# Expert rows added one pair behind their dots, and every fourth row of the first two chunks added by VectorE

## The chip, the cores and the metric

One core of a Trainium2 chip runs the whole program as one launch. The metric is the device time of one execution in microseconds. TensorE (PE in the profile) multiplies matrices, VectorE (DVE) and ScalarE (ACT) work on rows of 128 partitions, GpSimd (POOL) here only issues gathers, SyncE (SP) loads weights and stores the last result.

## The reference

Three layers on 512 tokens of width 1024, all in float32: a block with a short convolution and a block with a state-space mixer, each with a SwiGLU network, and then a hybrid layer: band attention and a gated delta rule side by side, and behind them a layer of retrieved experts (`peer`). The change concerns `peer` alone. For each token, 8 heads rank two sets of 128 keys, keep the 16 best sums each, and so name 128 experts out of 16384. Each expert is one pair of rows of 1024 numbers, `expert_down` and `expert_up`:

```
act = gelu(einsum("thkd,td->thk", expert_down[experts], hb))
y   = einsum("thk,thkd->td", gates * act, expert_up[experts])
out = x + gate2 * y
```

Tokens are handled in 4 chunks of 128. So there are 4 x 128 = 512 "rows" of work: row n = 128 c + s is the s-th expert of every token of chunk c, one expert per partition.

## The kernel before, in words

Everything ahead of the experts runs first. The hybrid layer is done in two halves of 256 tokens. Its second half (`main`, the generators `pe_main`, `act_main`, `dve_main` with f = 1) is cut into steps and woven into the expert loop, and so is the ranking of the keys for the next chunk (`ranks`, `dve_topk`): `steps_of` takes one or two steps of each a group. In chunk 0 that is one main step and two ranking steps, in chunk 1 one main step until these are used up and from then on a ranking step, in chunk 2 a ranking step, in chunk 3 none.

**One row.** `pool_gather` issues an indirect DMA of 128 x 2048 numbers (1 MB: the down and the up row of one expert for each token) into a slot. `dve_dots` multiplies the down half with the tokens' h (`htk`) and sums it, one custom instruction (L187), into a column of `dots`. `act_gelu` applies the gelu to both columns of a group (a group is GG = 2 rows, "a pair"). `dve_gate` multiplies with the gates (L170, 128x2). `act_diag` makes a 128x128 diagonal matrix of the result from the identity (L164, 128x128), one of 8 buffers. `pe_add` multiplies this matrix with the up half and adds it in PSUM (`acc`), two instructions in the code of 512 columns each, which the profile shows as four matmul records a row (L153, psum<-tail,arena 128x512).

**Slots.** For rows 0 to 255 there are NRING = 7 slots, from row 256 on 12, since memory of the main program has come free. A row's gather waits until TensorE has added the row that had the slot before (`g_mm.at(prev[n])`), 7 or 12 rows earlier.

**Order.** Every engine runs its own list; all wait by semaphores. Of one group, before the change:

```
VectorE: dve_dots(g)  steps_of(g)  dve_gate(g)
ScalarE: act_gelu(g)  steps_of(g)  act_diag(g)
TensorE:              steps_of(g)  pe_add(g)
```

At the end of a chunk `pe_finish` broadcasts the layer's gate (`gB`) and transposes x (`xo`) into PSUM, `act_finish` copies `gB` to `fin_out`, `dve_finish` multiplies it with `acc` and adds `xo`, and `store` writes it out (ScalarE for chunks 0 to 2, in the next chunk's group 4; SyncE for the last).

Helper lines carry all instructions: L153 matmul, L158 transpose, L164 activation, L170 tensor_tensor, L176 and L177 tensor_scalar, L182 scalar_tensor_tensor, L187 the dot, L216 the gather. "tail" is the memory of the hybrid layer (slots, dots, `fin_out`), "arena" holds among others the diagonal matrices and x.

Of the kernel before, what the change touches and what calls it, by code (L numbers as in the profile page):

```python
# [226 lines left out]
def build(nc, t, out):  # L227
    ctx = ExitStack()
    with ctx:
# [970 lines left out]
        def wait_steps(n):  # L1200
            for _ in range(n):
                yield
# [783 lines left out]
        def pe_tok(e, c):  # L1986
            for u in range(2):
                key = "htk", c, u
                o = ps.claim(key, QGB)
                e.wait_ge(*ps.vacant(key))  # L1990
                e.wait_ge(*t_h.at((5, c // 2, 7)))
                for k in range(4):
                    ins = e.tr(o[:, part[k]], H[:, 4 * u + k, part[c % 2]], ident)
                ins.then_inc(*tk_pe.tick((c, u)))
                yield
            yield

        def act_tok(e, c):
            yield
            for u in range(2):  # L2000
                e.wait_ge(*tk_pe.at((c, u)))
                if c > 1:
                    e.wait_ge(*g_dot.at(128 * (c - 2) + 127))
                e.act(htk[c % 2][:, 512 * u:512 * u + 512], ps["htk", c, u], ACT.Copy).then_inc(*ps.release(("htk", c, u)))
                yield
# [14 lines left out]
        def act_topk(e, c):  # L2020
            yield from wait_steps(31)
            e.wait_ge(*k_dve.at((c, "gate_in")))
            e.act(gates[c % 2], gates[c % 2], ACT.Exp).then_inc(*k_gate.tick(c))
            yield
# [130 lines left out]
        for n in range(512):  # L2155
            prev.append(last_use.get(slot_no[n]))
            last_use[slot_no[n]] = n
        g_in = landed("expert_landed", len(SLOTS))
        stored = landed("stored", 2)

        def pool_gather(e):
            for n in range(512):
                c, i = n // 128, n % 128
                e.wait_ge(*idx_ok.at(c))
                if prev[n] is not None:
                    e.wait_ge(*g_mm.at(prev[n]))
                e.gather(SLOTS[slot_no[n]], t["experts"], eidx[c % 2][:, i:i + 1]).then_inc(
                    *g_in.tick((c, i), slot_no[n]))

        def dve_dots(e, c, grp):  # L2170
            n = 128 * c + GG * grp
            d = dots[(n // GG) % 8]
            e.wait_ge(*ps.done(("htk", c, 1)))
            if n >= 8 * GG:
                e.wait_ge(*g_diag.at(n - 7 * GG - 1))
            for i in range(GG):
                s = SLOTS[slot_no[n + i]]
                e.wait_ge(*g_in.at((c, GG * grp + i)))
                e.ttr(s[:, 0:1024], s[:, 0:1024], htk[c % 2], d[:, i:i + 1]).then_inc(*g_dot.tick(n + i))
# [8 lines left out]
        def act_gelu(e, c, grp):  # L2188
            n = 128 * c + GG * grp
            d = dots[(n // GG) % 8]  # L2190
            e.wait_ge(*g_dot.at(n + GG - 1))
            e.act(d, d, ACT.Gelu).then_inc(*g_gelu.tick(n))

        def act_diag(e, c, grp):
            n = 128 * c + GG * grp
            d = dots[(n // GG) % 8]
            e.wait_ge(*g_act.at((c, grp)))
            for i in range(GG):
                if n + i >= 8:
                    e.wait_ge(*g_mm.at(n + i - 8))  # L2200
                e.act(diag[(n + i) % 8], ident, ACT.Copy, scale=d[:, i:i + 1]).then_inc(*g_diag.tick(n + i))

        def pe_add(e, c, grp):
            for i in range(GG):
                s_i = GG * grp + i
                n = 128 * c + s_i
                if s_i == 0:
                    for u in range(2):
                        ps.claim(("acc", c, u), (u,))
                        e.wait_ge(*ps.vacant(("acc", c, u)))  # L2210
                e.wait_ge(*g_in.at((c, s_i)))
                e.wait_ge(*g_diag.at(n))
                for u in range(2):
                    ins = e.mm(ps["acc", c, u], diag[n % 8], SLOTS[slot_no[n]][:, 1024 + 512 * u:1536 + 512 * u],
                               s_i == 0, s_i == 127)
                ins.then_inc(*g_mm.tick(n))

        def pe_finish(e, c):
            for u in range(2):
                o = ps.claim(("gB", c, u), HB)  # L2220
                e.wait_ge(*ps.vacant(("gB", c, u)))
                e.wait_ge(*der_ok.at((5, "post")))
                for k in range(4):
                    ins = e.mm(o[:, part[k]], post(5, 4 * u + k).broadcast_to([128, 128]), ident)
                ins.then_inc(*f_pe.tick(("gB", c, u)))
                o = ps.claim(("xo", c, u), HB)
                e.wait_ge(*ps.vacant(("xo", c, u)))
                for k in range(4):
                    ins = e.tr(o[:, part[k]], xT[:, 4 * u + k, 128 * c:128 * c + 128], ident)
                ins.then_inc(*f_pe.tick(("xo", c, u)))  # L2230

        def act_finish(e, c):
            for u in range(2):
                e.wait_ge(*f_pe.at(("gB", c, u)))
                if c:
                    e.wait_ge(*stored.at((c - 1, u)))
                e.act(fin_out[:, 512 * u:512 * u + 512], ps["gB", c, u], ACT.Copy).then_inc(*ps.release(("gB", c, u)))

        def dve_finish(e, c):
            e.wait_ge(*g_mm.at(128 * c + 127))  # L2240
            for u in range(2):
                f = fin_out[:, 512 * u:512 * u + 512]
                e.wait_ge(*ps.done(("gB", c, u)))
                e.tt(f, ps["acc", c, u], f, ALU.mult).then_inc(*ps.release(("acc", c, u)))
            for u in range(2):
                f = fin_out[:, 512 * u:512 * u + 512]
                e.wait_ge(*ps.done(("acc", c, u)))
                e.wait_ge(*f_pe.at(("xo", c, u)))
                e.tt(f, ps["xo", c, u], f, ALU.add).then_inc(*ps.release(("xo", c, u)))

        def store(e, c):
            for u in range(2):
                e.wait_ge(*ps.done(("xo", c, u)))
                e.dma(out[0, 128 * c:128 * c + 128, 512 * u:512 * u + 512], fin_out[:, 512 * u:512 * u + 512]).then_inc(
                    *stored.tick((c, u), u))
# [10 lines left out]
        def steps_of(c, grp, main, ranks):  # L2266

            if c == 0:
                some(ranks, 2)
                some(main, 2 if grp % 4 == 3 else 1)  # L2270
            elif c == 1 and next(main, True) is None:
                pass
            else:
                some(ranks, 1)

        def pe_experts(e):
            main = pe_main(e, 1)
            before_rows(main, iter(()))
            for c in range(4):
                ranks = iter(()) if c == 3 else wait_steps(32)  # L2280
                late = pe_tok(e, 3) if c == 2 else iter(())
                for grp in range(GROUPS):
                    steps_of(c, grp, main, ranks)
                    next(late, None)
                    pe_add(e, c, grp)
                pe_finish(e, c)

        def act_experts(e):
            main = act_main(e, 1)
            before_rows(main, iter(()))  # L2290
            drive(act_topk(e, 0))
            for c in range(4):
                ranks = iter(()) if c == 3 else act_topk(e, c + 1)
                late = act_tok(e, 3) if c == 2 else iter(())
                for grp in range(GROUPS):
                    act_gelu(e, c, grp)
                    steps_of(c, grp, main, ranks)
                    next(late, None)
                    if c and grp == 4:
                        store(e, c - 1)  # L2300
                    act_diag(e, c, grp)
                act_finish(e, c)

        def dve_experts(e, ranks):
            main = dve_main(e, 1)
            before_rows(main, ranks)
            drive(ranks)
            for c in range(4):
                ranks = iter(()) if c == 3 else dve_topk(e, c + 1)
                late = wait_steps(3) if c == 2 else iter(())  # L2310
                for grp in range(GROUPS):
                    dve_dots(e, c, grp)
                    steps_of(c, grp, main, ranks)
                    next(late, None)
                    dve_gate(e, c, grp)
                dve_finish(e, c)

# [228 lines left out]
```

## Time and profile before

| what | value |
|---|---|
| median of 3 runs | 3680.81 us (3666.36 to 3682.61) |
| the profiled execution | 3679.49 us, span 3677.7 us |
| PE busy | 3141.4 us (85%) |
| DVE busy | 2043.9 us (56%) |
| ACT busy | 1178.7 us (32%) |
| gathers | 512, 536.90 MB, first issued at 2100.36 us, last at 3640.8 us |
| row 0 dotted | 2106.76 us |
| row 128 dotted | 2656.70 us |
| row 256 dotted | 3032.26 us |

Times are microseconds from the start of the span. The expert loop takes up the last 1,578 us. Busy shares are those of an engine in a stretch; the idle time ahead of an instruction is given with what ended it. "DMA" is the mean busy share of the core's 16 DMA engines.

### The profile page before, as it was taken

The numbers are of one execution on the slowest core, as the hardware profiler recorded it, in microseconds if no ns is written. First come the engines' busy times: TensorE is split into PE (matmuls) and PEld (weight loads), VectorE is DVE, ScalarE is ACT, GpSimd is POOL, SyncE is SP. The second block draws the span as 40 slices with busy tenths as digits, with TensorE's granted clock in tenths as the row PEclk, the third lists the DMA queues.
The fourth block names the chain that finished last, engine by engine and source line by source line (L and its number), as shares of the span: only waits on it lengthen the run. The fifth ranks groups of instructions, "written<-read, shape, count | busy, mean of one in ns | idle before, by whom it ended". The sixth has DMA issues, their size and how long they took to land.

```text
span 3677.7 us, 34267 instructions
## 1 busy us (share of the span) xinstructions
PE 3141.4 (85%) x12402; PEld 2158.0 (59%) x12402; DVE 2043.9 (56%) x3974; ACT 1178.7 (32%) x2171; POOL 562.0 (15%) x540
## 2 busy tenths in 40 slices
PE   6989999798777989998988888977999777777777
PEld 4868888586555868886777635654565233223222
DVE  6654443776555454432552797554444878855554
ACT  3243222433444342223732345621222122211111
POOL 0000000000000000000000022212333444443332
PEclk9999999898888999998999989999999999999999
DMA  6534444242111424442303476867898999999998
GB/s 219 189 114 147 145 139 137 78 139 81 40 43 44 132 92 146 142 136 86 103 24 103 146 293 232 308 227 258 337 364 341 409 417 421 422 421 421 421 421 336
DMA packets 147543, 797.81 MB, mean 217 GB/s; under 512 B 16304, under 2 KB 18480, under 8 KB 81712
## 3 DMA queue, kind: packets, MB, share of 16 engines
q0 software_dynamic: 73728, 536.90, 36.8%
q1 hardware_dynamic: 69840, 251.69, 21.0%
q10 hardware_dynamic: 3808, 7.02, 0.5%
q8 instruction: 101, 1.65, 0.2%
q14 instruction: 66, 0.54, 0.0%
HBM read 793.46 MB, written 2.10 MB: 216 GB/s over the span
## 4 chain that ended last, share of the span: by engine, by line
PE 65%; DMA 17%; DVE 11%; ACT 4%; issue 3%; another core or an unknown queue 0%; POOL 0%; DVEq 0%; SPq 0%; ACTq 0%; POOLq 0%
PE psum L153 64%; DMA tail<-in_experts,tail 16%; DVE tail L187 2%; ACT arena L164 2%; DVE arena L182 2%; DVE tail L170 1%; ACT L164 1%; DVE tail L193 1%; PE psum L158 1%; DVE region L170 1%; DVE tail L190 1%; ACT region L164 1%; ACT tail L164 0%; DVE rounded L182 0%; DVE tail L196 0%
## 5 line engine op out<-in xcount | busy, mean ns | idle before, releaser
L153 PE MATMUL psum<-tail,arena 128*128 128x512 f32 (+2 forms) x3916 | 1386.7, 507 | 306.8 <-ACT arena L164 284.1
L153 PE MATMUL psum<-rounded,rounded 128*128 128x512 f32 x5496 | 1293.6, 396 | 40.1 <-DVE rounded L182 27.3
L153 PEld LDWEIGHTS psum<-tail,arena 128*128 128x128 f32 x3916 | 738.4, 196 | 916.8 <-issue 860.4
L153 PEld LDWEIGHTS psum<-rounded,rounded 128*128 128x128 f32 x5496 | 1036.6, 190 | 280.0 <-issue 56.2
L216 POOL DMA_INDIRECT tail<-in_experts,tail x512 | 541.9, 1058 | 1949.0 <-PE psum L153 977.9
L187 DVE CUSTOM_DVE_ANT_0 tail<-tail 128x1024 f32<-128x1024 f32 x512 | 621.4, 1225 | 351.7 <-DMA tail<-in_experts,tail 346.9
L170 DVE TENSOR_TENSOR rounded<-arena,rounded 128x1024 fp32r<-128x1024 f32 (+2 forms) x285 | 316.4, 1111 | 346.6 <-ACT rounded L164 346.4
L164 ACT ACTIVATE rounded<-arena 128x1024 fp32r<-128x1024 f32 (+2 forms) x317 | 291.9, 939 | 446.2 <-DVE arena L170 238.9
L164 ACT ACTIVATE tail<-tail 128x2 f32<-128x2 f32 (+1 forms) x288 | 64.1, 223 | 659.3 <-DVE tail L187 657.6
L164 ACT ACTIVATE arena<-arena,tail 128x128 f32<-128x128 f32 x512 | 177.6, 395 | 293.6 <-DVE tail L170 291.7
L164 ACT ACTIVATE arena<-psum 128x256 f32<-128x256 f32 (+2 forms) x210 | 97.8, 482 | 512.3 <-PE psum L153 512.0
L153 PE MATMUL psum<-arena 128*128 128x1 f32 (+3 forms) x792 | 197.6, 375 | 75.3 <-ACT arena L164 45.2
L164 ACT ACT_TABLE_LOAD x180 | 230.9, 1283 | 11.7 <-PE psum L153 6.4
L182 DVE SCALAR_TENSOR_TENSOR arena<-arena 128x512 f32<-128x512 f32 (+1 forms) x294 | 212.3, 724 | 21.7 <-ACT arena L164 10.9
L153 PEld LDWEIGHTS psum<-arena 128*128 128x128 f32 x792 | 127.5, 206 | 126.0 <-issue 82.1
L170 POOL TENSOR_TENSOR region<-region 128x256 f32<-128x256 f32 x24 | 19.9, 829 | 1130.6 <-DVE region L170 1130.6
L153 PE MATMUL psum<-tail 128*128 128x128 f32 (+4 forms) x888 | 138.9, 304 | 20.6 <-DVE tail L182 18.6
L153 PEld LDWEIGHTS psum<-tail 128*128 128x128 f32 (+2 forms) x888 | 108.8, 186 | 51.8 <-DVE tail L182 25.7
L170 DVE TENSOR_TENSOR arena<-psum,arena 128x512 f32<-128x512 f32 (+1 forms) x88 | 41.6, 476 | 168.2 <-PE psum L153 167.9
L182 DVE SCALAR_TENSOR_TENSOR arena<-psum,arena 128x511 f32<-128x511 f32 (+3 forms) x112 | 79.8, 713 | 97.2 <-PE psum L153 51.1
L170 DVE TENSOR_TENSOR tail<-tail 128x2 f32<-128x2 f32 (+5 forms) x299 | 95.7, 321 | 60.4 <-ACT tail L164 49.6
L164 ACT ACTIVATE arena<-arena 128x512 f32<-128x512 f32 (+3 forms) x138 | 80.6, 598 | 89.6 <-DVE arena L170 29.3
(82 smaller groups left out, 1452.5 us busy)
## 6 DMA issues: line engine op xcount, KB each, us to landing
arena<-in_ada SPq DMA_DIRECT2D x136, 512.0 KB
arena<-in_fin SPq DMA_DIRECT2D x88, 512.0 KB
arena<-in_win SPq DMA_DIRECT2D x56, 512.0 KB
arena<-in_fout SPq DMA_DIRECT2D x32, 512.0 KB
arena<-in_mxbc SPq DMA_DIRECT2D x32, 512.0 KB
arena<-in_pq SPq DMA_DIRECT2D x32, 512.0 KB
arena<-in_ain SPq DMA_DIRECT2D x24, 512.0 KB
arena<-in_mz SPq DMA_DIRECT2D x16, 512.0 KB
```

What stands on the lines that cost most here:

```text
L153: return self.e.matmul(o, a, b, start=start, stop=stop, skip_group_check=skip)
L158: return self.e.transpose(o, a, ident)
L164: return self.e.activation(o, a, func, bias=bias, scale=scale)
L170: return self.e.tensor_tensor(o, a, b, op)
L182: return self.e.scalar_tensor_tensor(out=o, in0=a, scalar=s, in1=b, op0=op0, op1=op1)
L187: return self.e.tensor_tensor_reduce(o, a, b, 1.0, 0.0, ALU.mult, ALU.add, total)
L190: return Unissued() if self.e is None else self.e.max(o, a)
L193: return Unissued() if self.e is None else self.e.max_index(o, m, a)
L216: return self.e.indirect_dma_start(out=o, out_offset=None, in_=table, in_offset=bass.IndirectOffsetOnAxis(ap=rows, axis=0))
```

## The change

Two things are done at once. First, `dve_gate`, `act_diag` and `pe_add` are called for the group before the one whose dots and steps are due, over chunk borders too, and on VectorE and ScalarE ahead of the steps. Second, `own_add(n)` names rows that VectorE adds itself: from slot 24 of a chunk on, every fourth row (s % 4 == 1) of chunks 0 and 1, and every sixteenth (s % 16 == 9) of chunks 2 and 3: 26, 26, 7 and 7 rows. It multiplies the up half with the column of `dots` and adds it to `fin_out` (`dve_add`, one scalar_tensor_tensor of 128x1024; the first of a chunk a tensor_scalar). The finish sums `acc` and `fin_out`, multiplies with `gB` straight from PSUM, and adds `xo`; `act_finish` is gone. The order of one group is now:

```
VectorE: dve_dots(g)  dve_gate(g-1)  dve_add(g-1)  [dve_finish(c-1) in a chunk's group 1]  steps_of(g)
ScalarE: act_gelu(g)  act_diag(g-1)  [store]  steps_of(g)
TensorE: steps_of(g)  pe_add(g-1)    [pe_finish(c-1) in a chunk's group 0]
```

The diff, cut to its core:

```diff
+        g_own = signal("expert_added_own")
+        def own_add(n):
+            s = n % 128
+            return s >= 24 and (s % 4 == 1 if n < 256 else s % 16 == 9)
+        by_pe = [n for n in range(512) if not own_add(n)]
+        turn = {n: i for i, n in enumerate(by_pe)}
+        added = lambda n: g_own.at(n) if own_add(n) else g_mm.at(n)
...
-                    e.wait_ge(*g_mm.at(prev[n]))
+                    e.wait_ge(*added(prev[n]))
...
+        def dve_add(e, c, grp):
+            for i in range(GG):
+                n = 128 * c + GG * grp + i
+                if not own_add(n):
+                    continue
+                v, g = SLOTS[slot_no[n]][:, 1024:2048], dots[(n // GG) % 8][:, i:i + 1]
+                e.wait_ge(*g_act.at((c, grp)))
+                before = [m for m in range(128 * c, n) if own_add(m)]
+                if before:
+                    e.wait_ge(*g_own.at(before[-1]))
+                    e.stt(fin_out, v, g, fin_out, ALU.mult, ALU.add).then_inc(*g_own.tick(n))
+                else:
+                    for u in range(2):
+                        e.wait_ge(*stored.at((c - 1, u)))
+                    e.ts(fin_out, v, g, ALU.mult).then_inc(*g_own.tick(n))
...
+            for u in range(2):
+                f = fin_out[:, 512 * u:512 * u + 512]
+                e.tt(f, ps["acc", c, u], f, ALU.add).then_inc(*ps.release(("acc", c, u)))
+            for u in range(2):
+                f = fin_out[:, 512 * u:512 * u + 512]
+                e.tt(f, ps["gB", c, u], f, ALU.mult).then_inc(*ps.release(("gB", c, u)))
...
+            for g, (c, grp) in enumerate(ALL_GROUPS):
+                steps_of(c, grp, main, ranks)
+                next(late, None)
+                if g:
+                    pe_add(e, *ALL_GROUPS[g - 1])
+                if g and grp == 0:
+                    pe_finish(e, c - 1)
+            pe_add(e, *ALL_GROUPS[-1])
+            pe_finish(e, 3)
...
+                act_gelu(e, c, grp)
+                if g:
+                    act_diag(e, *ALL_GROUPS[g - 1])
+                if c and grp == 4:
+                    store(e, c - 1)
+                steps_of(c, grp, main, ranks)
...
+                dve_dots(e, c, grp)
+                if g:
+                    dve_gate(e, *ALL_GROUPS[g - 1])
+                    dve_add(e, *ALL_GROUPS[g - 1])
+                if c and grp == 1:
+                    dve_finish(e, c - 1)
+                steps_of(c, grp, main, ranks)
```

## Rows read from the trace of the kernel before

**Rows 1.** The page: busy time of each engine; chain that ended last, by engine.
```profile
PE 3141.4 (85%) x12402; PEld 2158.0 (59%) x12402; DVE 2043.9 (56%) x3974; ACT 1178.7 (32%) x2171; POOL 562.0 (15%) x540
...
PE 65%; DMA 17%; DVE 11%; ACT 4%; issue 3%; another core or an unknown queue 0%; POOL 0%; DVEq 0%; SPq 0%; ACTq 0%; POOLq 0%
```
**Rows 2.** Busy time by stretch: length, PE, PEld, DVE, ACT, POOL, clock, DMA, GB/s.
```profile
2100.00:2264.00 164.00, 130.19 (x361) 64.22 (x360) 142.75 (x412) 79.83 (x146) 45.49 (x41) 0.84 0.71 263
2264.00:2640.00 376.00, 326.87 (x1304) 212.40 (x1303) 197.08 (x414) 129.75 (x257) 91.73 (x89) 0.95 0.77 281
2640.00:2656.00 16.00, 15.00 (x61) 8.97 (x59) 4.29 (x8) 3.02 (x7) 7.33 (x6) 1.00 0.97 386
2656.00:2805.00 149.00, 140.97 (x533) 92.80 (x533) 62.93 (x124) 39.17 (x118) 45.19 (x40) 0.98 0.90 337
2805.00:3017.00 212.00, 161.39 (x358) 65.69 (x359) 162.79 (x415) 45.33 (x136) 94.49 (x84) 0.97 0.99 403
3017.00:3665.00 648.00, 484.95 (x1088) 195.24 (x1087) 398.43 (x862) 121.33 (x393) 257.66 (x253) 0.98 1.00 417
```
**Rows 3.** Row adds on TensorE, by form, in 2264:2640, 2656:2805 and 2805:3017.
```profile
L153 PE MATMUL psum<-tail,arena 128*128 128x512 f32 x357 | 177.0, 643 | 47.8 <-ACT arena L164 47.8
...
L153 PE MATMUL psum<-tail,arena 128*128 128x512 f32 x160 | 76.0, 619 | 8.5 <-ACT arena L164 8.5
...
L153 PE MATMUL psum<-tail,arena 128*128 128x512 f32 x337 | 160.1, 621 | 50.6 <-ACT arena L164 50.6
```
**Rows 4.** Timeline of one pair in chunk 0: start, duration, [idle before <- releaser].
```profile
2403.48 0.70 ACT L164 ACTIVATE arena<-arena,tail 128x128 f32<-128x128 f32 x2 [0.83 <-DVE tail L170]
2404.03 3.67 PE L153 MATMUL psum<-tail,arena 128*128 128x512 f32 x8 [0.28 <-ACT arena L164]
```
**Rows 5.** Groups by form on VectorE, whole span.
```profile
L182 DVE SCALAR_TENSOR_TENSOR arena<-arena 128x512 f32<-128x512 f32 x270 | 203.8, 757 | 20.8 <-ACT arena L164 10.9 <-DMA arena<-in_ada 4.8
...
L182 DVE SCALAR_TENSOR_TENSOR tail<-tail,arena 128x256 f32<-128x256 f32 x24 | 10.3, 478 | 6.5 <-ACT arena L164 6.5
```
**Rows 6.** Timeline of a pair late in chunk 1.
```profile
2881.46 1.23 DVE L187 CUSTOM_DVE_ANT_0 tail<-tail 128x1024 f32<-128x1024 f32 x1 [0.82 <-DMA tail<-in_experts,tail]
...
2882.72 0.20 ACT L164 ACTIVATE tail<-tail 128x2 f32<-128x2 f32 x1 [2.50 <-DVE tail L187]
...
2884.51 0.70 ACT L164 ACTIVATE arena<-arena,tail 128x128 f32<-128x128 f32 x2 [1.58 <-DVE tail L170]
...
2887.29 1.18 POOL L216 DMA_INDIRECT tail<-in_experts,tail  x1 [2.32 <-PE psum L153]
```
**Rows 7.** Timeline: gathers of rows 173 and 142, and the dots that waited for them.
```profile
2799.41 0.94 POOL L216 DMA_INDIRECT tail<-in_experts,tail  x1 [4.16 <-PE psum L153]
...
2804.92 1.23 DVE L187 CUSTOM_DVE_ANT_0 tail<-tail 128x1024 f32<-128x1024 f32 x1 [1.75 <-DMA tail<-in_experts,tail]
...
2677.76 0.94 POOL L216 DMA_INDIRECT tail<-in_experts,tail  x1 [0.78 <-PE psum L153]
...
2690.30 1.23 DVE L187 CUSTOM_DVE_ANT_0 tail<-tail 128x1024 f32<-128x1024 f32 x1 [0.90 <-DMA tail<-in_experts,tail]
```
**Rows 8.** The dots by form in 2656:2805 and 2805:3017.
```profile
L187 DVE CUSTOM_DVE_ANT_0 tail<-tail 128x1024 f32<-128x1024 f32 x46 | 56.2, 1227 | 79.6 <-DMA tail<-in_experts,tail 79.6
...
L187 DVE CUSTOM_DVE_ANT_0 tail<-tail 128x1024 f32<-128x1024 f32 x81 | 98.8, 1227 | 42.8 <-DMA tail<-in_experts,tail 41.1 <-ACT arena L164 1.3
```
**Rows 9.** All that write or read in_experts, whole span.
```profile
DMA to landing us min/median/max: 14.3/22.9/24.8
```
**Rows 10.** Timeline of the end: the last pair on TensorE.
```profile
3666.64 3.67 PE L153 MATMUL psum<-tail,arena 128*128 128x512 f32 x8 [1.27 <-ACT arena L164]
```
**Rows 11.** Timeline: a gather beside a long VectorE instruction.
```profile
2211.53 2.98 POOL L216 DMA_INDIRECT tail<-in_experts,tail  x1 [0.78 <-PE psum L153]
...
2211.38 2.29 DVE L170 TENSOR_TENSOR tail<-tail 128x2048 f32<-128x2048 f32 x1
```
**Rows 12.** Who waited for whom on VectorE in 2264:2640: us, times, longest.
```profile
DVE tail L170 <- PE psum L153: 59.8, 26, 5.8
```

More of the change, by code:

```diff
@@ L2173, in dve_dots @@
             e.wait_ge(*ps.done(("htk", c, 1)))
-            if n >= 8 * GG:
-                e.wait_ge(*g_diag.at(n - 7 * GG - 1))
+            for m in range(n - 8 * GG, n - 7 * GG) if n >= 8 * GG else ():
+                e.wait_ge(*(g_own.at(m) if own_add(m) else g_diag.at(m)))
             for i in range(GG):
@@ L2198, in act_diag @@
             for i in range(GG):
-                if n + i >= 8:
-                    e.wait_ge(*g_mm.at(n + i - 8))
-                e.act(diag[(n + i) % 8], ident, ACT.Copy, scale=d[:, i:i + 1]).then_inc(*g_diag.tick(n + i))
+                if own_add(n + i):
+                    continue
+                k = turn[n + i]
+                if k >= 8:
+                    e.wait_ge(*g_mm.at(by_pe[k - 8]))
+                e.act(diag[k % 8], ident, ACT.Copy, scale=d[:, i:i + 1]).then_inc(*g_diag.tick(n + i))
         def pe_add(e, c, grp):
@@ L2206, in pe_add @@
                 n = 128 * c + s_i
+                if own_add(n):
+                    continue
                 if s_i == 0:
@@ L2213, in pe_add @@
                 for u in range(2):
-                    ins = e.mm(ps["acc", c, u], diag[n % 8], SLOTS[slot_no[n]][:, 1024 + 512 * u:1536 + 512 * u],
+                    ins = e.mm(ps["acc", c, u], diag[turn[n] % 8], SLOTS[slot_no[n]][:, 1024 + 512 * u:1536 + 512 * u],
                                s_i == 0, s_i == 127)
@@ L2230, in pe_finish @@
                 ins.then_inc(*f_pe.tick(("xo", c, u)))
[L2232 to L2237, printed above, removed]
+        def dve_add(e, c, grp):
+            for i in range(GG):
+                n = 128 * c + GG * grp + i
+                if not own_add(n):
+                    continue
+                v, g = SLOTS[slot_no[n]][:, 1024:2048], dots[(n // GG) % 8][:, i:i + 1]
[8 more added lines that the diff above has]
+                    e.ts(fin_out, v, g, ALU.mult).then_inc(*g_own.tick(n))
         def dve_finish(e, c):
             e.wait_ge(*g_mm.at(128 * c + 127))
+            e.wait_ge(*g_own.at(max(n for n in range(128 * c, 128 * c + 128) if own_add(n))))
+            for u in range(2):
[3 more added lines that the diff above has]
+                f = fin_out[:, 512 * u:512 * u + 512]
+                e.wait_ge(*ps.done(("acc", c, u)))
+                e.wait_ge(*f_pe.at(("gB", c, u)))
+                e.tt(f, ps["gB", c, u], f, ALU.mult).then_inc(*ps.release(("gB", c, u)))
             for u in range(2):
@@ L2243, in dve_finish @@
                 e.wait_ge(*ps.done(("gB", c, u)))
[L2244 to L2247, printed above, removed]
                 e.wait_ge(*f_pe.at(("xo", c, u)))
@@ L2274, in steps_of @@
                 some(ranks, 1)
+        ALL_GROUPS = [(c, grp) for c in range(4) for grp in range(GROUPS)]
         def pe_experts(e):
@@ L2278, in pe_experts @@
             before_rows(main, iter(()))
[L2279 to L2286, printed above, removed]
+            for g, (c, grp) in enumerate(ALL_GROUPS):
+                if grp == 0:
+                    ranks = iter(()) if c == 3 else wait_steps(32)
+                    late = pe_tok(e, 3) if c == 2 else iter(())
+                steps_of(c, grp, main, ranks)
[6 more added lines that the diff above has]
+            pe_finish(e, 3)
         def act_experts(e):
@@ L2291, in act_experts @@
             drive(act_topk(e, 0))
[L2292 to L2302, printed above, removed]
+            for g, (c, grp) in enumerate(ALL_GROUPS):
+                if grp == 0:
+                    ranks = iter(()) if c == 3 else act_topk(e, c + 1)
+                    late = act_tok(e, 3) if c == 2 else iter(())
+                act_gelu(e, c, grp)
[4 more added lines that the diff above has]
+                steps_of(c, grp, main, ranks)
+                next(late, None)
+            act_diag(e, *ALL_GROUPS[-1])
         def dve_experts(e, ranks):
@@ L2307, in dve_experts @@
             drive(ranks)
[L2308 to L2316, printed above, removed]
+            for g, (c, grp) in enumerate(ALL_GROUPS):
+                if grp == 0:
+                    ranks = iter(()) if c == 3 else dve_topk(e, c + 1)
+                    late = wait_steps(3) if c == 2 else iter(())
+                dve_dots(e, c, grp)
[5 more added lines that the diff above has]
+                steps_of(c, grp, main, ranks)
+                next(late, None)
+            dve_gate(e, *ALL_GROUPS[-1])
+            dve_add(e, *ALL_GROUPS[-1])
+            dve_finish(e, 3)
         def sp_program(e):
```

## The prediction

> **What bounds the kernel now.** I began with the page. TensorE is busy for 85% of the span and holds 65% of the chain that ended last; the DMA holds 17% of it, VectorE 11% [rows 1]. Such shares mix stages, and the diff touches one stage alone, the last 1,578 us, in which 512 expert rows are gathered, dotted and added. So the second view was the busy time by stretch, cut where the work changes [rows 2]. The reader should see five regimes there.
>
> - 2100 to 2264 (rows 0 to 38 of chunk 0): VectorE is busy 142.75 of 164 us; it ranks keys for chunk 1 two steps a pair. VectorE is the bound.
> - 2264 to 2640 (rows 38 to 127): TensorE 326.87 of 376 us; the DMA engines 77%. TensorE is nearly the bound.
> - 2640 to 2656, the change of chunk: VectorE works only 4.29 of 16 us, TensorE 15.00.
> - 2656 to 2805 (40 rows of chunk 1, beside the query projection): TensorE 140.97 of 149, DMA 90%.
> - From 2805 on the main program is used up and the DMA is 99 to 100% busy: the gathers are the bound, first with 7 ring slots (to 3017), then with 12.
>
> The third view was the groups by form in three of these stretches. In 2264 to 2640 TensorE's idle time ahead of the 128x512 row adds is 47.8 us [rows 3]; the window leaves 376 - 327 = 49 us of idle in all. So practically all of it is one wait, that for the scaled identity from ScalarE. The timeline shows how it comes about: ScalarE makes it at 2403.48, 0.83 us late for VectorE's gate, and TensorE starts the two rows at 2404.03 and needs 3.67 us [rows 4]. That gate stands behind a whole step of the main program on VectorE.
>
> **What the reordering does.** A pair's gate, scaled identity and add come one pair later, when the gelu has long been done. In 2264 to 2640 that takes the 47.8 us wait away from TensorE. It also gives one of every four rows (from slot 24 on) to VectorE. A row costs TensorE 3.67/2 = 1.8 us [rows 4]. Slots 41 to 125 in steps of 4 are 22 rows: 22 x 1.8 = 40 us less on TensorE. Its floor is then 327 - 40 = 287 us. But the DMA has 0.77 x 376 = 290 us of work there [rows 2], so no ordering can gain more than 86 us.
>
> VectorE pays with one scalar_tensor_tensor of 128x1024. No row shows this size; 128x512 takes 757 ns and 128x256 478 ns [rows 5], so 1024 columns come to 757 + 2 x 279 = 1315 ns, say 1.3 us. Not less than a dot of the same width (1.23 us [rows 6]), not more than 2 x 0.757 = 1.5. Per pair that is 0.65 us on an engine that is half idle here.
>
> **The price: the ring.** Rows below 256 live in 7 slots, and a slot is given back when its row is added, now one pair later. The loop, from steady rows: the second dot ends 1.23 us after 2881.46, at 2882.69; the gelu ends at 2882.92. In the new order the gate of the pair before was free to run at 2882.7, so its scaled identity can start at about 2883.0. From its start to the gather that its first add lets go takes 2887.29 - 2884.51 = 2.8 us [rows 6]. So dots end to next gather: 3.1 us. That gather (row n + 7) must land, and be dotted (1.2 us), two pairs later, which gives a period T = (3.1 + 1.2 + L) / 2 per pair, L being the time from gather to landing. L is 5.5 us at its lowest (2799.41 to a dot that waited for it at 2804.92) and 12.5 us in a crowd (2677.76 to 2690.30) [rows 7]. So T lies between 4.9 and 8.4 us. The old order kept one more pair of slots in flight, which is the reserve that is spent.
>
> **Sum by stretch.**
> 1. 2100 to 2264: VectorE idles 21 us of 164. Rows 25, 29, 33 and 37 add 4 x 1.3 = 5 us to it; some waits go. Between +5 and -16; taken -5.
> 2. 2264 to 2640: 357 matmul records [rows 3] at 4 a row are 89 rows, 44.6 pairs of 8.4 us. Between the floor of 290 us (-86) and no gain. I take 7.25 us a pair, 324 us, so -52: 5.9 to 6.9 by the loop above for L of 7.5 to 9.5 (weight loads share the queues), and something for VectorE, which now does dots, gate and own add in one piece (2.5 + 0.15 + 0.65 = 3.3 us) ahead of the step that TensorE's next step needs.
> 3. 2640 to 2656: the final sums of a chunk move behind two pairs of dots, so VectorE's 11.7 idle us shrink; TensorE has 1 us of idle there and a few in the restart. Taken -3 (0 to -8).
> 4. 2656 to 2805: 160 records [rows 3], 40 rows, 10 of them VectorE's: 10 x 1.8 = 18 us less on TensorE. The DMA's own work is 0.90 x 149 = 134 us [rows 2], so at most -15. Taken -8.
> 5. 2805 to 3017: nothing to gain, since the DMA is 99% busy [rows 2]. 337/4 = 84 rows [rows 3], 42 pairs of 5.05 us. With L at 5.5, T is 4.9, just enough; with L at 7.5 it is 5.9, at 10 it is 7.15. As soon as T passes 5 us the queues empty and L falls to its low value, and VectorE (162.79 of 212 us busy) gains 20 own adds, 26 us. Taken 5.4 us, so +15; ends 0 and +88. What is late next there are the dots, which already wait 41.1 us for landings [rows 8].
> 6. 3017 on, 12 slots: gathers land 22.9 us after issue in the median [rows 9] against 5.5 alone, so some 17 us is queueing. Holding a slot a pair (5 us) longer eats 5 of these 17; the DMA stays full: 0. VectorE's 14 own adds (18 us) fit in its 250 idle us. If that cover went, they would cost up to 18.
> 7. The end: the last pair now waits for the one before, 3.67 us of TensorE's time [rows 10], two more 128x512 sums on VectorE, less one copy of ScalarE: +4.
>
> Sum: -5 - 52 - 3 - 8 + 15 + 0 + 4 = -49. The profiled execution took 3679.5 us (span 3677.7 and 1.8 around it), and the median of the runs is 3680.8. So 3630.5, rounded to 3630 us.
>
> **A rule against the change.** A gather that starts beside a long VectorE operation is stretched: 2.98 us at 2211.53, beside a 2.29 us tensor_tensor from 2211.38; its usual time is 0.94 [rows 11], and one started near the end of a dot took 1.18 [rows 6]. The Trainium skill (SBUF — State Buffer, Who interferes with whom) says that a VectorE instruction with two SBUF inputs contends with a GpSimd instruction that reads SBUF, which fully blocks. By that rule, the trace agrees, each own add can hold up a gather for all its length. I take it as hidden, since own adds come right after the gate and the gathers some 3 us later; it is rival D.
>
> **Rivals.**
> A. The floors are reached: stretches at -16, -86, -3, -15, 0, 0, +4, sum -116: 3564 us. For it: nearly all of TensorE's idle is the wait removed. Against: TensorE and DMA would both have to be full at once.
> B. The ring becomes the bound, slower than before. Place: chunk 1 after 2805, with L near 10 us as in a full queue. Price: T = 7.15, +88 there, the middle only 7.9 us a pair (-24), head and start 0, end +4: +68, 3748 us. It decides from a tail loss of 64 us on (the other terms come to -64), that is T = 6.6, L = 8.9 us. For it: the gather at 2677.76 took 12.5 us [rows 7]. Against: it was issued while three others were still under way, which a longer hold forbids.
> C. The wait only moves: TensorE's next main step then waits for VectorE's or ScalarE's step instead of the scaled identity. Middle -10, tail +5, end +4: 3679 us, no change. For it: VectorE in its turn waits 59.8 us for TensorE there [rows 12], so part of the stretch is a chain and not a full engine. Against: TensorE has only 49 us of idle in it.
> D. Own adds block gathers: 42 of them in stretches 2 and 5 at 1.3 us each, 55 us: 3685 us.
>
> **Chances.** The forecast 0.55 (3600 to 3655 by itself), A 0.15, B 0.12, C 0.11, D 0.02, and 0.05 for a smaller gain than forecast. Under 0.5% (18 us) nothing can be told in this kernel, whose three runs lie 16 us apart. Faster 0.75, same 0.13, slower 0.12. The range goes from 3575, in A, to 3690, past C and D.
>
> **What the profile after would show.** Right: in the 128x512 row adds of chunk 0, TensorE's idle ahead of them falls from 48 to under 15 us; row 127's dot comes some 55 us earlier; own adds of about 1.3 us; pairs of 5.2 to 5.7 us in the tail of chunk 1 with the DMA below 97%; 2.5 us a row from 3017 on. Wrong: if the dots wait for landings all through chunk 0 (B), if new waits of TensorE on VectorE's steps appear (C), or if gathers of 2 us stand beside own adds (D). The number most likely to be off is T in stretch 2, then T in stretch 5.

## The result and the profile after

The changed kernel takes 3691.28 us (median of 10 runs, 3683.14 to 3698.36) against 3678.82 us of the kernel before in the same session: a ratio of 1.0035, with a 95% interval from 1.0024 to 1.0046. It is 0.35% slower, within the 0.5% that I had called no change, 61 us above the 3630 us that I had forecast and just past 3690 us, the upper end of my range. The profiled execution took 3689.87 us with a span of 3687.9.

The busy time by stretch, cut at the same places as [rows 2] (length, PE, PEld, DVE, ACT, POOL, clock, DMA share, GB/s):

```profile
2100.00:2264.00 164.00, 119.09 (x335) 58.33 (x333) 139.71 (x399) 73.30 (x134) 41.93 (x38) 0.83 0.67 245
2264.00:2640.00 376.00, 321.75 (x1296) 216.82 (x1296) 250.05 (x484) 131.35 (x259) 113.37 (x99) 0.91 0.83 314
2640.00:2656.00 16.00, 11.27 (x32) 5.56 (x31) 8.15 (x19) 5.67 (x17) 6.92 (x6) 1.00 0.98 352
2656.00:2805.00 149.00, 136.70 (x526) 90.76 (x525) 66.09 (x131) 32.34 (x103) 44.13 (x42) 0.95 0.94 351
2805.00:3017.00 212.00, 134.67 (x213) 50.70 (x211) 168.06 (x388) 25.27 (x90) 85.20 (x71) 0.81 0.93 345
```

Two lines tell the story. In the second, VectorE and the DMA have done more between 2264 and 2640 than in [rows 2] (99 gathers against 89), and TensorE, in slightly less busy time (321.75 us against 326.87), has got further with the main program: 302 of its 1296 matmul records are row adds, against 357 of 1304 before. In the last, everything has got thinner: 71 gathers against 84, the DMA from 99% to 93%, TensorE's granted clock from 0.97 to 0.81. The kernel gains in the middle of chunk 0 and gives it back behind it.

Windows mix work once the time has shifted, so from here on a stretch is named by rows and runs from the start of one row's dot on VectorE to the start of another's, read from each timeline. The part ahead of row 0 is the same code in all kernels and ended between 2106.7 and 2115.5 us in their profiled executions, so stretches are compared, and totals by the medians. A profiled execution is one of several and can lie off the median (3679.49 us for 3678.82 and 3689.87 for 3691.28 in these two). In us:

| rows | before | after (difference) | my steps |
|---|---|---|---|
| 0 to 40 | 181.2 | 192.4 (+11) | -5 |
| 40 to 128 | 368.7 | 320.1 (-49) | -52 - 3 |
| 128 to 172 | 145.2 | 153.2 (+8) | -8 |
| 172 to 248 | 200.3 | 229.3 (+29) | +15 |
| 248 to 511 | 662.1 | 668.7 (+7) | 0 |
| last dot to the end | 13.3 | 17.4 (+4) | +4 |
| sum | | +10 | -49 |

The groups by form for 2264:2640 answer to [rows 3]: first TensorE's row adds, then the dots on VectorE.

```profile
L153 PE MATMUL psum<-tail,arena 128*128 128x512 f32 x302 | 153.0, 646 | 28.8 <-ACT arena L164 27.8 <-DVE tail L170 1.0
...
L187 DVE CUSTOM_DVE_ANT_0 tail<-tail 128x1024 f32<-128x1024 f32 x100 | 121.5, 1225 | 100.7 <-DMA tail<-in_experts,tail 100.7
L182 DVE SCALAR_TENSOR_TENSOR tail<-tail 128x1024 f32<-128x1024 f32 x24 | 30.8, 1285 | 0.9
```

TensorE's idle ahead of its adds fell from 47.8 to 28.8 us. The dots now wait 100.7 us for landings. In the kernel before, the same stretch had:

```profile
L187 DVE CUSTOM_DVE_ANT_0 tail<-tail 128x1024 f32<-128x1024 f32 x89 | 106.1, 1224 | 19.8 <-DMA tail<-in_experts,tail 19.8
```

The own add takes 1285 ns, as forecast (1.3 us). The same view for 2805:3017, to be held against [rows 3, 8]:

```profile
L153 PE MATMUL psum<-tail,arena 128*128 128x512 f32 x213 | 135.1, 790 | 76.0 <-ACT arena L164 75.9
...
L187 DVE CUSTOM_DVE_ANT_0 tail<-tail 128x1024 f32<-128x1024 f32 x70 | 85.0, 1222 | 37.9 <-DMA tail<-in_experts,tail 37.6
```

Here TensorE's idle grew from 50.6 to 76.0 us, with over a third of its add records gone (213 against 337), and one of them takes 790 ns instead of 621. The timeline late in chunk 1, against [rows 6], in order of time:

```profile
2853.51 1.23 DVE L187 CUSTOM_DVE_ANT_0 tail<-tail 128x1024 f32<-128x1024 f32 x1 [1.23 <-DMA tail<-in_experts,tail]
...
2854.85 1.28 DVE L182 SCALAR_TENSOR_TENSOR tail<-tail 128x1024 f32<-128x1024 f32 x1
2854.89 0.39 ACT L164 ACTIVATE arena<-arena,tail 128x128 f32<-128x128 f32 x1
2855.41 1.54 POOL L216 DMA_INDIRECT tail<-in_experts,tail  x1 [1.87 <-PE psum L153]
2855.42 1.96 PE L153 MATMUL psum<-tail,arena 128*128 128x512 f32 x4 [0.28 <-ACT arena L164]
...
2857.65 0.94 POOL L216 DMA_INDIRECT tail<-in_experts,tail  x1 [0.70 <-PE psum L153]
...
2860.63 0.68 ACT L164 ACTIVATE arena<-arena,tail 128x128 f32<-128x128 f32 x2
...
2861.16 5.37 PE L153 MATMUL psum<-tail,arena 128*128 128x512 f32 x8 [3.78 <-ACT arena L164]
...
2865.40 1.23 DVE L187 CUSTOM_DVE_ANT_0 tail<-tail 128x1024 f32<-128x1024 f32 x1 [2.00 <-DMA tail<-in_experts,tail]
```

The reader should see the loop of the prediction. The second dot of a pair (row 199's) ends at 2853.51 + 1.23 = 2854.74; the row added for the pair before lets a gather go at 2857.65, 2.9 us later; that gather brings row 203, whose dot has waited 2.00 us when it starts at 2865.40, 7.75 us after the gather. And a pair of adds that took 3.67 us before takes 5.37 here (2861.16).

### The profile page after: what moved, and what is told of

It is laid out like the page before. It is cut to its first block, busy times and chain, and to the rows that moved or that the text cites. A ratio compares the mean times of both kernels' runs of the same rounds, so it can differ in the third digit from the quotient of the medians.

```text
span 3687.9 us, 33721 instructions
## 1 busy us (share of the span) xinstructions
PE 3092.1 (84%) x12138; PEld 2135.9 (58%) x12138; DVE 2120.4 (57%) x4048; ACT 1129.1 (31%) x2097; POOL 598.1 (16%) x540
## 4 chain that ended last, share of the span: by engine, by line
PE 62%; DMA 19%; DVE 11%; ACT 4%; issue 3%; POOL 0%; DVEq 0%; SPq 0%; ACTq 0%
PE psum L153 61%; DMA tail<-in_experts,tail 19%; DVE tail L187 3%; ACT arena L164 2%; DVE arena L182 2%; DVE tail L170 1%; ACT L164 1%; DVE tail L182 1%; PE psum L158 1%; DVE tail L193 1%; DVE region L170 1%; ACT region L164 1%; DVE tail L190 1%; DVE rounded L182 0%; DVE arena L177 0%
## 5 line engine op out<-in xcount | busy, mean ns | idle before, releaser
L153 PE MATMUL psum<-tail,arena 128*128 128x512 f32 (+2 forms) x3652 | 1333.2, 519 | 336.6 <-ACT arena L164 309.1
L153 PEld LDWEIGHTS psum<-tail,arena 128*128 128x128 f32 x3652 | 713.8, 204 | 916.6 <-issue 852.4
L216 POOL DMA_INDIRECT tail<-in_experts,tail x512 | 578.0, 1129 | 1923.9 <-DVE tail L199 949.5
L164 ACT ACTIVATE arena<-arena,tail 128x128 f32<-128x128 f32 x446 | 154.6, 387 | 0.0
L153 PE MATMUL psum<-region 128*64 128x128 f32 (+2 forms) x560 | 79.0, 362 | 33.7 <-DVE region L170 32.8
```

Source lines behind the costliest of these rows:

```text
L153: return self.e.matmul(o, a, b, start=start, stop=stop, skip_group_check=skip)
L164: return self.e.activation(o, a, func, bias=bias, scale=scale)
L216: return self.e.indirect_dma_start(out=o, out_offset=None, in_=table, in_offset=bass.IndirectOffsetOnAxis(ap=rows, axis=0))
```

## The experiments

All ratios are against the kernel before in the same session (its medians: 3678.0 to 3680.8 us). Stretches are from the one profiled execution of each kernel.

Two theories. **R, the ring:** one pair more of holding a slot costs wherever the 7 slots have no reserve, whoever adds the rows. **C, own adds:** the rows given to VectorE load it and thin TensorE's work, so that its clock falls, its adds take longer, and slots come back late. For C speaks the fall of the clock that the last row of the first view shows.

### The two parts alone

`order_alone`: no row is VectorE's, the rest of the change stays (with ScalarE's copy of the gate row in the finish, called in group 1).

```diff
-            return s >= 24 and (s % 4 == 1 if n < 256 else s % 16 == 9)
+            return False
```

> Only the order: gates, diagonals and adds one pair behind, all rows added by TensorE, the finish with ScalarE's copy as in the kernel before. Theory R (the longer hold of the 7 slots): the loss in the late part of chunk 1 stays, 5.8 to 6.1 us a pair between rows 172 and 248 against 5.3 in the kernel before, rows 0 to 40 again 11 us late, rows 40 to 128 some 30 us faster; about 3700 us in all. Theory C (VectorE's own adds: they load VectorE, and they thin TensorE's work so that its clock falls and its adds take 5.4 us a pair): late chunk 1 at 5.1 to 5.4 us a pair with the granted clock back above 0.9, about 3680 us.

Measured 3694.79 us, ratio 1.004 (1.0026 to 1.0055). Rows 172 to 248 took 229.2 us, 6.03 us a pair; rows 0 to 40 191.5, rows 40 to 128 319.0, rows 128 to 172 161.5 (16 more than before).

`own_alone`: VectorE's own adds, in the order of the kernel before.

```diff
-                if g:
-                    dve_gate(e, *ALL_GROUPS[g - 1])
-                    dve_add(e, *ALL_GROUPS[g - 1])
                 steps_of(c, grp, main, ranks)
                 next(late, None)
+                dve_gate(e, c, grp)
+                dve_add(e, c, grp)
```
(and likewise `act_diag` and `pe_add` of the same group behind the steps, the finish at the end of the chunk)

> Only VectorE's own adds, in the order of the kernel before (gate, then own add, behind the steps). Theory R: late chunk 1 at 5.3 us a pair as before, rows 0 to 40 unchanged, rows 40 to 128 some 35 us faster since TensorE loses 22 rows; about 3640 us. Theory C: late chunk 1 at 5.8 us a pair with the granted clock near 0.8; about 3660 us.

Measured 3651.17 us, ratio 0.9925 (0.9903 to 0.9947). Rows 40 to 128 took 341.2 us (-27.5), 128 to 172 141.5 (-3.7), 172 to 248 203.6 (5.36 a pair). Busy time of rows 172 to 248 in `order_alone`, then in `own_alone`:

```profile
2787.00:3016.00 229.00, 156.68 (x320) 62.55 (x320) 156.15 (x402) 38.11 (x124) 92.91 (x77) 0.93 0.94 349
```
```profile
2768.00:2971.00 203.00, 134.86 (x258) 54.22 (x257) 178.43 (x421) 37.32 (x108) 96.91 (x78) 0.86 0.98 393
```

The first has the clock back at 0.93 and is as slow as the changed kernel; the second has it at 0.86, VectorE busier by 22 us, and the DMA at 98%. Theory C is refuted as the cause of the loss in these rows. R's numbers hold for these rows in both kernels (5.8 to 6.1 expected and 6.03, 5.3 and 5.36); the gain of own adds in rows 40 to 128 was 27.5 us and not 35, and the total came out 11 us above the 3640 expected.

### Both parts in places

In the following kernels a function `behind(g)` says for each pair whether it is handled one pair later or in its own turn.

`own_while_main`: the changed kernel, every fourth row VectorE's only up to row 171.

```diff
-            return s >= 24 and (s % 4 == 1 if n < 256 else s % 16 == 9)
+            return s >= 24 and (s % 4 == 1 if n < 172 else s % 16 == 9)
```

> The changed kernel, but every fourth row is VectorE's only up to row 171, where the main program ends; behind it every sixteenth. Theory R: late chunk 1 still 5.8 us a pair or more, about 3685 us. Theory C: 5.1 to 5.4 us a pair there, clock above 0.9, about 3662 us.

Measured 3690.46 us, 1.0028 (1.0016 to 1.0039); rows 172 to 248 233.9 us, 6.15 a pair, clock 0.89. Thinning out the own adds bought nothing in this order.

`both_while_main`: the same rows, and `behind(g)` is `g < 86`.

> Both parts of the change while the main program lasts (pairs 0 to 85, rows up to 171); from there on the order of the kernel before and every sixteenth row for VectorE. Theory R: late chunk 1 back at 5.3 us a pair, rows 0 to 40 still 11 us late, rows 40 to 128 49 us faster as in the changed kernel; about 3650 us, faster than both kernels. Theory C says the same of this kernel as of the one before it in this list, 3662 us. If both are wrong, and the 12-slot part simply takes what was gained, it stays near 3680 us.

Measured 3647.8 us, 0.9912 (0.9878 to 0.9947); rows 172 to 248 back at 201.3 us. Only the order from row 172 on differs from `own_while_main`: 43 us in the medians. But it is not to be told from own adds alone, because the order costs in rows 0 to 40 (189.9 against 177.8) and 128 to 172 (153.3 against 141.5) most of what it gains in 40 to 128 (311.2 against 341.2).

`middle_behind`: own adds as in the changed kernel, `behind(g)` is `20 <= g < 64`.

> VectorE's own adds as in the changed kernel, one pair behind only for pairs 20 to 63 of chunk 0 (rows 40 to 127), the order of the kernel before elsewhere. Theory R (the order costs wherever a pair is short against the time of a landing, and pays only where TensorE waited for ScalarE's diagonal): the stretches of the earlier runs add up, 178 us for rows 0 to 40, 316 for 40 to 128, 142 for 128 to 172, 204 for 172 to 248, 662 to the last dot, 13 behind it: 3622 us. If the order's gain in rows 40 to 128 is only work put off to later (rival: conservation by the DMA), rows 128 to 172 take 150 us or more and the total stays at the 3651 of own adds alone.

Measured 3633.37 us, 0.9867 (0.9849 to 0.9884); rows 0 to 40 177.9, 40 to 128 317.8, 128 to 172 148.9, 172 to 248 209.0. 18 us under own adds alone, 11 over the expectation: rows 128 to 172 and 172 to 248 took 7 and 5 us longer than in `own_alone`. The profiled execution was the slowest of the four (3645.61 us). The rival, that the gain in rows 40 to 128 is only put off, wanted 150 us or more in rows 128 to 172 and a total of 3651: the total speaks against it, but the 148.9 us leave room for some of it, and what makes these two stretches longer no run isolates.

`middle_behind_own172`: the same with own adds thinned from row 172 on.

> As middle_behind, but from row 172 on only every sixteenth row is VectorE's. Theory R with VectorE's load as a small term: rows 172 to 248 take 201 us instead of 204, 3620 us in all; if the fall of the clock matters (0.86 against 0.92 there) they take 5 us less or more.

Measured 3629.08 us, 0.9859 (0.9837 to 0.988), an interval that overlaps with that of `middle_behind`; rows 172 to 248 202.5, with the clock at 0.91 against 0.84. That is 6.5 us less than in `middle_behind`, past the 5 us that I had written down as the sign that the clock matters. VectorE's load was cut by the same edit, so the run does not tell the two apart.

`late_behind`: own adds as in the changed kernel, `behind(g)` is `g >= 128`.

> VectorE's own adds as in the changed kernel, one pair behind only from row 256 on, where there are 12 slots. My step on this stretch said 0, and +4 at the end: then rows 248 to 511 take 662 us as with own adds alone and the rest 17 us, 3655 us in all. If holding slots longer costs with 12 slots too, rows 248 to 511 take 668 us, as they did in the changed kernel, and it comes to 3661 us.

Measured 3653.99 us, 0.9932 (0.9911 to 0.9953); rows 248 to 511 661.8 us, the end 16.4. With 12 slots the order costs nothing but its +3 at the end.

### The size of the ring, and which row of a pair is moved

`six_all_behind` and `six_own_alone`: the changed kernel and `own_alone` with one slot fewer for rows 0 to 255 (and 11 instead of 12 behind them), one run each, so without an interval.

```diff
-        NRING = (WORDS - LOW - t_at[0]) // 2048
+        NRING = 6
```

> The changed kernel with 6 slots instead of 7 for rows 0 to 255 (11 instead of 12 behind). Theory R: the loop of slot, landing and dots gets 1.72 us or more longer per two pairs, so rows 40 to 128 take 345 us or more (320 with 7) and rows 172 to 248 260 us (229 with 7). If the slots didn't bound, both stay.

> VectorE's own adds in the order of the kernel before, with 6 slots instead of 7. Theory R: this order has a pair of slots in reserve, so rows 40 to 128 lose little (341 with 7 slots, up to 350), rows 172 to 248 some (204 with 7, 215), and with 6 slots it is faster than the order one pair behind in every stretch.

Measured 3865.03 and 3687.65 us. One slot costs the order one pair behind 174 us and the old order 36. In rows 40 to 128 the first went from 320.1 to 371.7 us, the second from 341.2 to 349.4, so that the gain of the reordering there has turned into a loss; rows 172 to 248 288.4 and 226.2 us, both above what I expected. VectorE's waits for landings in 2300:2800 of `six_all_behind` (us, times, longest):

```profile
DVE tail L187 <- DMA tail<-in_experts,tail: 197.8, 75, 11.6
```

`middle_even`: `middle_behind`, but VectorE takes the first row of a pair.

```diff
-            return s >= 24 and (s % 4 == 1 if n < 256 else s % 16 == 9)
+            return s >= 24 and (s % 4 == 0 if n < 256 else s % 16 == 8)
```

> As middle_behind, but the row that VectorE takes is the first of its pair (s % 4 == 0), not the second. With the order one pair behind, rows 40 to 128 took 319 us with and without own adds, so not TensorE's work but the return of slots bounds them, says theory R; the first row of a pair lets the next gather go, so giving it to VectorE, which adds it some 3 us sooner, should take 5 to 15 us off rows 40 to 128. If TensorE's chain of steps bounds them, nothing changes: 316 to 320 us.

Measured 3613.63 us, 0.9812 (0.9793 to 0.9831); rows 40 to 128 301.5 us, 16 less than in `middle_behind` with as many rows moved. Waits in 2300:2600 of `middle_behind`, then of `middle_even`:

```profile
DVE tail L187 <- DMA tail<-in_experts,tail: 75.0, 39, 5.6
```
```profile
DVE tail L187 <- DMA tail<-in_experts,tail: 56.9, 36, 3.3
...
POOL tail L216 <- DVE tail L182: 12.5, 9, 2.6
```

The gathers now wait in nine places for VectorE's own add instead of for TensorE, and the dots wait less for landings.

`all_behind_even`: the changed kernel with that same edit.

> The changed kernel with one difference: VectorE takes the first row of a pair (s % 4 == 0, in chunks 2 and 3 s % 16 == 8). If the return of the slots bounds the order one pair behind, rows 40 to 128 take about 302 us instead of 320, and rows 172 to 248 come from 229 to 215 us or less: 3660 us in all. If TensorE's or VectorE's load were the bound, nothing would change against the changed kernel, 3691 us, since as many rows are moved as there.

Measured 3666.45 us, 0.9973 (0.9961 to 0.9984), 25 us under the changed kernel. Rows 40 to 128 304.4 us, as expected; rows 172 to 248 233.7, where I had expected 215. A miss: there only every second pair has its first row taken, and the loop through the other pairs stays. The same is true of rows 40 to 128, though, where the edit gained 16 us, so this alone does not explain it; the cause is open.

`middle_even_own172`: `middle_even` with own adds thinned from row 172 on.

> The best of what the runs showed, put together: one pair behind for rows 40 to 127 alone, VectorE takes the first row of every second pair up to row 171, and behind that one row in sixteen. Rows 40 to 128 as in middle_even, 302 us; 128 to 172 143; 172 to 248 202; 3610 us in all, 0.981 of the kernel before.

Measured 3610.58 us, 0.9818 (0.9804 to 0.9831), and 299.0, 147.9 and 201.2 us in the three stretches of the expectation: 1.8% faster than the kernel before, 2.2% faster than the changed one, and not to be told from `middle_even`. These two are the best kernels of the study.

## Why the prediction was wrong, step by step

**The loop was right, two of its terms were not, and I did not ask for it in rows 0 to 40 and 128 to 172.** I had T = (3.1 + 1.2 + L) / 2 per pair. From each pair of the timelines I took x, from the end of a pair's dots to the gather that the first add of the pair before lets go, and L, from that gather to the dot of its row (so L holds what the landed row waits for VectorE, too):

| kernel, rows | x | L | pairs in which the gather waited for its slot and the dot for that landing | us a pair |
|---|---|---|---|---|
| before, 40 to 128 | 2.8 | 12.7 | 7 of 44 | 8.38 |
| after, 40 to 128 | 5.5 | 8.0 | 34 of 44 | 7.27 |
| before, 128 to 172 | 4.6 | 7.8 | 21 of 22 | 6.60 |
| after, 128 to 172 | 5.3 | 7.3 | 21 of 22 | 6.96 |
| before, 172 to 248 | 0.2 | 9.0 | 24 of 38 | 5.27 |
| after, 172 to 248 | 3.8 | 7.1 | 27 of 38 | 6.04 |
| order_alone, 172 to 248 | 3.3 | 7.5 | 35 of 38 | 6.03 |

(x + L + 1.2) / 2 comes to the measured us a pair by itself, since x, L and the dot make up the time from the end of one pair's dots to the end of those two pairs later. That sum is therefore no test of the loop. The column of pairs that waited twice is one, and so is the ring of 6 slots.

**Step 5, 172 to 248: +15 forecast, +29 measured.** I took 5.4 us a pair, which means L = 6.5. I argued that the queues empty as soon as T passes 5 us and L falls to its low value. It fell from 9.0 to 7.1 and 7.5 and no lower, with the DMA still 93% busy; what keeps it there no run isolates. x was 3.3 with the order alone and 3.8 in the changed kernel, where the adds were slower. One us of L or x is half a us a pair. My base was low as well: 5.05 us a pair counts 84 rows by TensorE's adds, while [rows 8] have 81 dots in that window, and by the dots of rows 172 to 248 the kernel before took 5.27, so that my 5.4 would have been +5 us there. Mechanism right, size off.

**Step 4, 128 to 172: -8 forecast, +8 measured.** Here the step was wrong in kind. I weighed TensorE's work against the DMA's and did not ask for the loop. But the loop already bound 21 of 22 pairs there before the change, and TensorE does its main step first and the add behind it, so x is not 3.1 but 5.3 us (4.6 before), and a pair took 7.0 us against 6.6. `order_alone` took 161.5 us there, 16 more than before, `own_alone` 141.5, 4 less: the order is what costs.

**Step 1, rows 0 to 40: -5 forecast, +11 measured**, the same omission. I reckoned that VectorE was the bound and had time for waits to go. One place in the changed kernel, where TensorE works through a long step of the main program ahead of its adds (gather, then the dot that waits for it):

```profile
2278.21 0.94 POOL L216 DMA_INDIRECT tail<-in_experts,tail  x1 [12.18 <-PE psum L153]
```
```profile
2283.89 1.23 DVE L187 CUSTOM_DVE_ANT_0 tail<-tail 128x1024 f32<-128x1024 f32 x1 [9.11 <-DMA tail<-in_experts,tail]
```

GpSimd waits 12.18 us for a slot, and VectorE then 9.11 us for the row. By the average of 9 us a pair there was reserve; but among these pairs one takes 23.5 us in the kernel before (from row 38's dot to row 40's) and 25.5 in the changed one. `own_alone` and `middle_behind`, which leave the order alone in these rows, took 177.8 and 177.9 us, `order_alone` 191.5.

**Steps 2 and 3, 40 to 128: -55 forecast, -49 measured.** 7.27 us a pair against the 7.25 taken. That the number fits so well is in part luck: L was 8.0, within my 7.5 to 9.5, but x was 5.5 and not 3.1, and my sum covered this only by the unspecified addition for VectorE. The two sources that I had named do not add up, though. Order alone gives -49.7 us, own adds alone -27.5, both together -48.6. Once the wait for the diagonal is shorter, the ring bounds the stretch (34 of 44 pairs), and 40 us less on TensorE buy nothing; to gain from both, the rows moved must be those that free a slot earlier (`middle_even`, -67).

**Step 6, the 12 slots: 0 forecast, +7 measured between rows 248 and 511.** `late_behind` has the order there and shows 0 for it, so the step holds for the 12 slots. The 7 us lie where the 7 slots give way to the 12: rows 248 to 272 took 68.1 us against 62.6 before, and rows 272 to 511 600.7 against 599.5. The first eight rows were even faster (24.7 against 30.0); rows 256 to 260 took 16.1 us against 8.1. `order_alone` took 68.1 us for rows 248 to 272 as well, `own_alone` 62.6 and `late_behind` 61.2, so it is the order ahead of row 256 that costs there; by which wait, I did not follow up.

**Step 7, the end: +4, and +4 measured.**

**The rivals.** B, the ring as the bound, described what happened in its place and mechanism, with 29 us instead of 88; its tail did not decide alone, but the same loop in the rows where I had not looked for it did. A did not come about: no stretch reached its floor. C's 'no change' (3679 us) fits the result, but mostly for the wrong reason: TensorE's waits for VectorE in 2264:2640 did rise, from 0.6 to 17.4 us, but the waits of the dots for landings rose from 19.8 to 100.7. D was named with a price of 55 us: gathers are stretched by own adds (1.54 us at 2855.41, beside the own add that ends at 2856.13), but none of 2 us stands beside one, and the mean of all 512 gathers was 1.13 us (1.06 before) with own adds and without them (`order_alone`). `own_alone`, with all 66 of these adds, was 30 us faster than the kernel before. The Trainium skill (SBUF — State Buffer, Who interferes with whom) has the rule, and the trace agrees that it acts; it costs little here.

Of what I said the profile would show, TensorE's idle fell to 28.8 and not under 15 us, row 127's dot came 28.8 us earlier and not some 55, own adds, the DMA below 97% in the tail and 2.5 us a row from 3017 on were right, 6.04 us a pair was outside my 5.2 to 5.7, and 'if the dots wait for landings all through chunk 0 (B)' was what one saw.

## What to carry to other kernels

When a consumer is moved one step later, write down the loop slot - transfer - use - release for every stretch in which the ring is in use, with the longest step that now stands between use and release, and not just for the stretch that the DMA bounds already. With few slots the average period is no guide; one slot more or fewer shows at once how near the edge a kernel is (174 us here). Taking work off a full engine pays only as long as this loop is not the bound, and then it matters which item is moved: the one whose release comes first.

## What the runs showed of the hardware

TensorE's mean granted clock in rows 172 to 248 was 0.97 in the kernel before (busy 154 of 200 us), 0.93 with the order alone (157 of 229), 0.86 with own adds alone (135 of 204) and 0.80 with both (146 of 229); with both, a pair of row adds took 5.37 us in one place against 3.67 before. In the order one pair behind, this left no trace in the time, which I had not expected: 6.04 us a pair at 0.80 and 6.03 at 0.93, since x was 0.5 us longer and L 0.4 us shorter. In the old order that is not shown: with fewer own adds from row 172 on, the clock went from 0.84 to 0.91 and these rows from 209.0 to 202.5 us (`middle_behind` and `middle_behind_own172`), and from 0.83 to 0.92 and from 205.9 to 201.2 in the two `middle_even` kernels, but VectorE had less to do as well.

What stretches a gather can be read from the traces. In the kernel before, all 13 gathers that started within a 128x2048 tensor_tensor on VectorE, which reads two tiles, ended 0.81 to 0.84 us after it and so took 1.1 to 2.98 us. In the changed kernel, 11 of the 14 that started within an own add ended about 0.8 us after it, as the one at 2855.41 did (2855.41 + 1.54 = 2856.95, against 2856.13), and the other 3, which had started within 0.06 us of the own add's start, took the usual 0.94. Dots hold gathers up too: 96 of them in the kernel before, up to 1.99 us long. The 7 that started there within a tensor_reduce, which reads one tile, took 0.94 us.
